# Gate and up products of two feed-forward layers in seven block products instead of eight, and a last norm by features

## What is computed

```python
def rmsnorm(t, g):
    tf = t.astype(jnp.float32)
    y = tf * lax.rsqrt(jnp.mean(tf * tf, axis=-1, keepdims=True) + EPS)
    return (y * g.astype(jnp.float32)).astype(t.dtype)
...
        hffn = modulate(rmsnorm(x, g_norm2[l]), shift2, scale2)
        a, u = jnp.split(jnp.einsum('bsd,df->bsf', hffn, w_ffn_in[l]), 2, axis=-1)
        x = x + gate2[:, None, :] * jnp.einsum('bsf,fd->bsd', jax.nn.silu(a) * u, w_ffn_out[l])

    return rmsnorm(x, g_final)
...
        h = rmsnorm_2(x, norm_ffn[l])
        x = x + (jax.nn.silu(h @ w_ffn_gate[l]) * (h @ w_ffn_up[l])) @ w_ffn_down[l]
    return rmsnorm_2(x, norm_final)
```

## Time and profile before

| | |
|---|---|
| median of 3 runs | 1884.28 us (1883.42 to 1884.56) |
| the profiled execution | 1884.31 us |
| its span, first to last instruction | 1882.5 us |
| TensorE matmul busy | 1847.2 us, 98% |
| TensorE weight load busy | 1435.2 us, 76% |
| VectorE busy | 833.8 us, 44% |
| ScalarE busy | 681.7 us, 36% |
| GpSimd busy | 570.5 us, 30% |
| granted TensorE clock | 0.996 of full |

### The profile page before, as it was taken

How to read it: one execution, slowest core, us unless ns; L and a number is a source line. 1 busy time by engine, 2 the same in 40 slices (tenths; PEclk the granted TensorE clock), 3 DMA queues, 4 the chain that set the end, 5 groups by cost and what they waited for, 6 DMA issues and landing times.

```text
span 1882.5 us, 21005 instructions
## 1 busy us (share of the span) xinstructions
PE 1847.2 (98%) x8472; PEld 1435.2 (76%) x8472; DVE 833.8 (44%) x1232; ACT 681.7 (36%) x1007; POOL 570.5 (30%) x437
## 2 busy tenths in 40 slices
PE   5999999999999999999999999999999999999998
PEld 3777778878777777877888888877776788888886
DVE  6666561425151303334333333548777654423433
ACT  4555552223232323433221222535546532212323
POOL 4643344646365544431000000044556211100100
PEclk9999999999999999999999999999999999999999
DMA  7422112534443122333422322432221222223321
GB/s 286 146 68 68 59 59 95 202 134 164 149 135 112 64 71 85 129 99 90 133 82 91 111 90 70 110 95 80 89 90 57 79 90 89 90 91 92 106 84 54
DMA packets 153299, 192.37 MB, mean 102 GB/s; under 512 B 10297, under 2 KB 130377, under 8 KB 152818
## 3 DMA queue, kind: packets, MB, share of 16 engines
q1 hardware_dynamic: 151202, 181.77, 29.4%
q0 software_dynamic: 1104, 5.24, 1.0%
q10 hardware_dynamic: 896, 4.01, 0.6%
HBM read 188.89 MB, written 4.72 MB: 103 GB/s over the span
## 4 chain that ended last, share of the span: by engine, by line
PE 93%; DVE 4%; ACT 2%; issue 1%; DMA 0%; ACTq 0%; SPq 0%; DVEq 0%
PE bank L1478 26%; PE bank L1483 25%; PE bank L1480 25%; PE bank L1503 2%; PE bank L1501 2%; PE bank L1499 2%; PE bank L1578 2%; PE bank L1512 2%; DVE stg L1794 1%; PE bank L1528 1%; PE bank L1548 1%; PE bank L1564 1%; DVE left L1824 1%; PE bank L1727 1%; PE bank L1706 1%
## 5 line engine op out<-in xcount | busy, mean ns | idle before, releaser
L1478 PE MATMUL bank<-hH,wh 128*128 128x512 f32 x1264 | 519.5, 411 | 3.3 <-ACT hH L2186 3.0
L1483 PE MATMUL bank<-hL,wh 128*128 128x512 f32 x1264 | 501.7, 397 | 0.1
L1480 PE MATMUL bank<-hH,wl 128*128 128x512 f32 x1264 | 501.1, 396 | 0.0
L2573 POOL TENSOR_TENSOR wl<-stg,wh 128x512 fp32r<-128x512 f32 x150 | 202.5, 1350 | 772.8 <-ACT wh L2212 772.6
L2212 ACT ACTIVATE wh<-stg 128x1024 fp32r<-128x1024 f32 (+2 forms) x292 | 298.7, 1025 | 270.2 <-PE bank L1483 190.5
L1478 PEld LDWEIGHTS bank<-hH,wh 128*128 128x128 f32 x1264 | 238.4, 189 | 76.4 <-issue 23.3
L1483 PEld LDWEIGHTS bank<-hL,wh 128*128 128x128 f32 x1264 | 238.3, 189 | 58.2 <-DVE hL L1938 0.5
L1480 PEld LDWEIGHTS bank<-hH,wl 128*128 128x128 f32 x1264 | 239.0, 189 | 53.8 <-issue 2.6
L1785 DVE TENSOR_TENSOR wl<-stg,wh 128x1024 fp32r<-128x1024 f32 (+2 forms) x142 | 168.3, 1188 | 239.8 <-ACT wh L2212 239.3
L2574 POOL TENSOR_TENSOR wl<-stg,wh 128x512 fp32r<-128x512 f32 x150 | 204.2, 1361 | 0.0
L1478 PE MATMUL bank<-h2H,wh 128*128 128x512 f32 x352 | 140.6, 399 | 0.0
(11 more groups left out here) (319 smaller groups left out, 2525.4 us busy)
## 6 DMA issues: line engine op xcount, KB each, us to landing
stg<-in_w_in SPq DMA_DIRECT2D x54, 1024.0 KB, 5.2
stg<-in_w_ada_t SPq DMA_DIRECT2D x48, 512.0 KB, 4.4
stg<-in_w_ffn_in SPq DMA_DIRECT2D x22, 1024.0 KB, 5.1
stg<-in_w_ffn_gate SPq DMA_DIRECT2D x11, 1024.0 KB, 5.3
stg<-in_w_ffn_up SPq DMA_DIRECT2D x11, 1024.0 KB, 5.3
stg<-in_w_ffn_down SPq DMA_DIRECT2D x10, 1024.0 KB, 5.1
stg<-in_w_proj_ret SPq DMA_DIRECT2D x8, 1024.0 KB, 5.1
stg<-in_w_out SPq DMA_DIRECT2D x8, 1024.0 KB, 5.2
```

The costliest lines, as they stand in the source:

```text
L1478: T.matmul(ps, wh, xh, start=j["first"] and k == 0, stop=False)
L1480: T.matmul(ps, wl, xh, start=False, stop=False)
L1483: t = T.matmul(ps, wh, xl, start=False, stop=j["stop"] and last)
L2573: G.tensor_tensor(lo[:, 0:h, :], src[:, 0:h, :], hi[:, 0:h, :], ALU.subtract)
```

## The change

Of the 44 blocks of gate and up weights, the first gate and the first up block of each layer stay as they were. The other 40 (called groups) are done as two by two blocks. A group's weights are cut into four corners of 512 input features (the even or the odd tiles) by 128 output features, the activations into four quarters of 512 input features by 256 tokens. Seven products of a corner, or of a sum of corners (S1 to S4), with a quarter, or a sum of quarters (T1 to T4), stand in place of eight. Each product is 4 tiles of input features times 3 matmuls of 256 columns, 84 matmuls in a group in place of 48 of 512 columns.

- The sums T1 to T4 are made once in each layer (`combine`: VectorE, 128x1024 each, with high and low part), from an unsplit copy of the activations (`HF`, named `ha` and `hb`), which ScalarE writes in 8 more operations of 128x512 in each layer.
- VectorE makes S1 to S4 of each group (128x512 each) into three PSUM banks of rings Z and C. The weight parts `wh` and `wl` are now six buffers of 128x512, one for each product's weights: the high part by ScalarE, the low part by GpSimd for plain corners (products 1, 2 and 4) and by VectorE for sums (3, 5, 6 and 7).
- Products 1, 6, 7 and 4 of a group pile up in one half bank ("own"), and between them VectorE adds what stands there to what ScalarE copied from products 2, 3 and 5 ("other" bank). So product 6 may begin when VectorE has read the bank after product 1, and so on. Own products of one group alternate with products 2, 5 and 3 of the next, or, at a lot's end, with the first down jobs.
- silu, the factor `RT` and the product of gate and up run on rows of 512 tokens, of which the second row is done in halves of 256.
- The down products of tag "b" have features on the partitions as in tag "a". The 32 transposes, `XT` and the norm by rows are gone. ScalarE squares each feature tile, VectorE adds the squares, a matmul with a constant matrix gives the mean, two ScalarE operations of 128x512 give the factor (`factor("n5")`), and `y` scales eight tiles: six on VectorE, two on GpSimd. The output leaves the chip as features by tokens and is turned on the host.

The core of the diff:

```diff
+FAST = "ab"
+QUADS = {1: "11", 2: "12", 3: "S4", 4: "22", 5: "S1", 6: "S2", 7: "S3"}
...
+    def combine(tag):
+
+        for i in range(1, 5):
+            p.tick("v_t", "T", tag, i)
+            emit("combo", tag, i)
+            yield
+            p.split_high(("T", tag), i)
+            emit("combo_high", tag, i)
+            yield
+            yield
+            p.split_low(("T", tag), i, "dve")
+            emit("combo_low", tag, i)
+            yield
...
+        def fast(lot, groups, tail):
+
+            items = [(groups[0], 2), (groups[0], 5), (groups[0], 3)]
+            for g, nxt in zip(groups, groups[1:] + [None]):
+                for e, (own, other) in enumerate(((1, 2), (6, 5), (7, 3))):
+                    items += [(g, own), (nxt, other) if nxt is not None else tail[e]]
...
+            def prepare():
...
+                for which in {5: (1,), 3: (2, 4), 7: (3,)}.get(m, ()):
+                    add(g, which)
+                p.quads[g, m] = {"u": len(p.units)}
+                p.units.append(("quad", g, m))
+                p.n_hi += 1
+                p.quads[g, m]["hi"] = p.n_hi
+                emit("quad_high", g, m)
+                state["low"] = (g, m)
...
+            def product(g, m):
+                if m == 1:
+                    take("G", ("own", g), 0)
+                elif m == 2:
+                    take("G", ("other", g), 0)
+                for k in range(KT // 2):
+                    emit("mult", g, m, k)
+                    p.slot()
+                p.gemms += 1
+                p.mults[g, m] = p.gemms
+                if m == 4:
+                    emit_out(g, 2)
+                    give(("own", g))
+                    return
+                if m != 3:
+                    p.tick("v_c" if m in (1, 6, 7) else "a_c", "C", g, m)
+                emit("part", g, m)
+                if m == 3:
+                    give(("other", g))
+                if m == 6:
+                    emit_out(g, 1)
...
+            halves = [(f2, x0) for f2 in range(4) for x0 in (0, nf // 2)]
+            if groups:
+                halves[1], halves[2] = halves[2], halves[1]
+            for f2, x0 in halves:
+                b = p.block(wd, f2 * 256, k0=f0 + x0, kn=nf // 2)
+                for half in range(2):
+                    p.job(b, half, down_job(lot, 2 * f2 + half, x0, x0 == 0, x0 > 0), x=("f" + tag, lot),
+                          x0=x0, n=nf // 2, first=x0 == 0, stop=x0 > 0, lo=lo)
...
-        WH = [sb(f"wh{i}", [P, 1024], F32R) for i in range(3)]
-        WL = [sb(f"wl{i}", [P, 1024], F32R) for i in range(3)]
+        WH = sb("wh", [P, 6, S], F32R)
+        WL = sb("wl", [P, 6, S], F32R)
...
+            def mult(g, m, k):
...
+                t_of = {4: 4, 5: 1, 6: 2, 7: 3}.get(m)
+                if t_of is None:
+                    c0 = 256 if m == 3 else 0
+                    tile, of_x = 2 * k + (m != 1), (x, 2 * k + (m != 1))
+                    xh, xl = (y[:, c0:c0 + 256] for y in operand(x, tile))
+                else:
+                    of_x = ("T", tag), t_of
...
+                        ticked(pe, "C", g, {6: 1, 7: 6, 4: 7, 5: 2, 3: 5}[m])
+                pe.wait_ge("w_hi", quads[g, m]["hi"])
+                high_done(pe, *of_x)
+                T.matmul(ps, wh[:, k, :], xh, start=k == 0 and m in (1, 2, 5), stop=False, skip_group_check=True)
+                pe.wait_ge(*quads[g, m]["lo"])
+                T.matmul(ps, wl[:, k, :], xh, start=False, stop=False, skip_group_check=True)
+                low_done(pe, *of_x)
+                t = T.matmul(ps, wh[:, k, :], xl, start=False, stop=k == KT // 2 - 1, skip_group_check=True)
+                if k == KT // 2 - 1:
                     t.then_inc(s["gemm"], 1)
...
+            def combo(tag, i):
...
+                out, x, y = {1: (F[:, 0], b12, b11), 2: (F[:, 1], b22, F[:, 0]), 3: (F[:, 0], b22, b12),
+                             4: (F[:, 0], b21, F[:, 1])}[i]
...
+            def sum_(g, which):
...
+                if which == 1:
+                    x, y, op = corner(g, 1, 2), corner(g, 2, 2), ALU.add
+                elif which == 2:
+                    ticked(ve, "S", g, 1)
+                    ve.wait_ge("w_hi", quads[g, 5]["hi"])
+                    x, y, op = sum_of(g, 1), corner(g, 1, 1), ALU.subtract
+                elif which == 3:
+                    x, y, op = corner(g, 1, 1), corner(g, 1, 2), ALU.subtract
+                else:
+                    ticked(ve, "S", g, 2)
+                    x, y, op = corner(g, 2, 1), sum_of(g, 2), ALU.subtract
+                V.tensor_tensor(sum_of(g, which), x, y, op).then_inc(s["v_s"], 1)
+
+            def quad_low(g, m):
+                if QUADS[m][0] == "S":
+                    src, hi, lo = quad_of(g, m)
+                    ve.wait_ge("w_hi", quads[g, m]["hi"])
+                    V.tensor_tensor(lo, src, hi, ALU.subtract).then_inc(s["w_lo_dve"], 1)
...
+            def part(g, m):
+
+                if m in (1, 6, 7):
+                    other = {1: 2, 6: 3, 7: 5}[m]
+                    ve.wait_ge("gemm", mults[g, m])
+                    if m == 6:
+                        emptied(ve, ("other", g))
+                    else:
+                        ticked(ve, "C", g, other)
+                    V.tensor_tensor(kept(g, other), half_of(g, m), kept(g, other), ALU.add).then_inc(s["v_c"], 1)
...
+            def out_row(g, row):
+                x, dst = groups[g], row_of(g, row)
+                if x["which"] == "u":
+                    ticked(ve, "out", x["mate"], row)
+                    if row == 1:
+                        ticked(ve, "C", g, 6)
+                        V.tensor_tensor(dst[:, :], dst[:, :], TMP[4 + 2 * (g % 2)][:, :], ALU.mult).then_inc(s["v_f"], 1)
+                    else:
+                        emptied(ve, ("own", x["mate"]))
+                        ve.wait_ge("gemm", mults[g, 4])
+                        V.tensor_tensor(dst[:, 0:256], half_of(g, 4), dst[:, 0:256], ALU.mult).then_inc(empty(("own", g)), 1)
+                        ticked(ve, "C", g, 7)
+                        V.tensor_tensor(dst[:, 256:512], dst[:, 256:512], kept(g, 5), ALU.mult).then_inc(s["v_f"], 1)
+                elif x["tag"] == "b" and row == 2:
+                    row_free(ve, g, row)
+                    ve.wait_ge("gemm", mults[g, 4])
+                    V.tensor_tensor(dst[:, 0:256], half_of(g, 4), RT[:, 0:256], ALU.mult).then_inc(empty(("own", g)), 1)
+                    ticked(ve, "C", g, 7)
...
+            def y():
+                r5 = factor("n5")
+                for f in range(2, KT):
+                    emptied(ve, ("down", "b", 1, f))
+                    t = V.scalar_tensor_tensor(XR[:, f, :], XR[:, f, :], C("norm_final_2", f), r5[:, :], ALU.mult, ALU.mult)
...
+                    if key == "n5":
+                        A_.activation(RT[:, :], log[:, :], ACTF.Exp, scale=-0.5).then_inc(s["a_r5"], 1)
+
+            def y_scale(f):
+                emptied(ac, ("down", "b", 1, f))
+                A_.activation(TMP[f][:, :], XR[:, f, :], ACTF.Copy, scale=C("norm_final_2", f)).then_inc(s["a_y"], 1)
...
+            def quad_high(g, m):
+                src, hi, _ = quad_of(g, m)
+                q = QUADS[m]
+                if q[0] == "S":
+                    ticked(ac, "S", g, 4 if q == "S2" else int(q[1]))
+                else:
+                    landed(ac, g)
+                released(ac, quads[g, m]["u"] - 6)
+                A_.activation(hi, src, ACTF.Copy).then_inc(s["w_hi"], 1)
...
+            def part(g, m):
...
+                    x = groups[g]
+                    ac.wait_ge("gemm", mults[g, m])
...
+                    t = A_.activation(kept(g, m), half_of(g, m), ACTF.Copy)
+                    t.then_inc(empty(("other", g)) if m == 3 else s["a_c"], 1)
...
+            def row_scale(g, row):
+                dst = row_of(g, row)
+                ticked(po, "silu", g, row)
+                G.tensor_tensor(dst[:, :], dst[:, :], RT[:, :], ALU.mult).then_inc(s["p_f"], 1)
...
+            def y():
+                po.wait_ge("a_y", 2)
+                po.wait_ge("a_r5", 1)
+                for f in range(2):
+                    G.tensor_tensor(XR[:, f, :], TMP[f][:, :], RT[:, :], ALU.mult).then_inc(s["p_y"], 1)
```

582 lines of the change are left out of this document (388 added, 194 removed).

## The result

The changed kernel takes 1957.03 us (median of 4 runs, 1956.37 to 1958.87), the kernel before 1884.42: ratio 1.039, interval 1.038 to 1.040. 1848 was forecast, 1836 to 1886 the range. It is 72.6 us slower where 36 us less were expected: 109 us lie between.

A forecast was written before the change was run, and what follows sets the result against it. TensorE was taken as the bound, with VectorE nearly as busy and setting the second layer's pace. Ten pairs a layer, 199 + 210 = 409 against 450.0 us, save 41.0; 1884.3 - 41.0 + 4.4 = 1847.7, say 1848 us, range 1836 to 1886.

The forecast's parts named there:

- TensorE's step: Start to start of 256-column matmuls in gate and up groups: 0.1172 us taken, 3360 x 0.1172 = 393.8 us, 56.2 less.
- A fixed cost: Rival: a fixed cost in each matmul makes the 256-column step 0.126 us, 1872 us in all; 20%.
- no addition at all: Rival: the 256-column step is 0.111 us and VectorE sets the pace in both layers, 1835 us; 5%.
- loads that don't hide: Slower rival: weight loads no longer hide under matmuls; 1943 us at a step of 0.150, about 2070 at 0.188; 13%.
- 0.2 us a pair for bunches: First layer's pairs of groups: allowance for TensorE waiting on VectorE's readings, added to TensorE's 19.7 us a pair.
- 5% of idle time: Second layer's pairs: VectorE sets the pace, its in-order list of 20.0 us plus 5% for waits gives 21.0 us.
- The slack of 1.4 us: Block products: TensorE waits on VectorE's readings one product ahead, leaving 12 x 0.117 = 1.4 us.
- GpSimd's hold: VectorE operations reading two tiles outside PSUM are delayed by GpSimd: 1.6 us a pair in the first layer, 2.7 in the second.
- The edits around: Outside block products: transposes -3.5, down products +0.6, sums T1 to T4 and lot openings +2, end +5.3; sum +4.4 us.
- The end: From the last matmul's end to the span's end: 12.0 us in place of 6.7, 5.3 us more.
- VectorE or its quarrel with GpSimd costs more: Rival: waits double and stall each group, 21.0 us a pair in the first layer, 22.5 in the second, 1874 us; 13%.
- near 90%: Sign in the changed profile: VectorE's busy share in the second layer, where it was to set the pace.

The follow-up runs named there:

- Experiments 1, 5 and 6: Changed kernel with weight sums one item earlier (1927.7 us); with ScalarE's half of finished rows one product later (1947.48 us); with both (1905.29 us).
- spread: Experiment 7's kernel with VectorE's sums S2 and S4 moved behind the next group's first reading and preparations spread evenly: 1889.36 us.
- experiment 7: Kernel with both moves of experiment 6, plus the first down block's high and low part prepared ahead of each lot's end: 1887.45 us.
- halves: Seven products in both layers, first layer ordered as in experiment 7, second as in spread, with GpSimd's low parts in two operations of 256 columns: 1875.54 us.
- tail_only: Changed kernel with both FFNs in whole products as before, only the last down product and last norm changed: 1879.54 us.

## Why the prediction was wrong

- **TensorE's step, right.** 0.1172 us was taken; the median is 0.117. A fixed cost, no addition at all and loads that don't hide, on which three rivals and 38% hung, did not come up. The prediction named this step as what it would be wrong in above all, with "all else" at a fifth of it; all of the error lay in that rest. The estimate by the Trainium skill (TensorE: Matmul & The Clock Gate, Back-to-back issue gap), 109 ns, was 8 ns low.
- **The sentence that failed:** "In the first layer I allow 0.2 us a pair for bunches", and "I add 5% of idle time" in the second. It adds each engine's work, takes the longest, and leaves a small allowance for lists that wait for each other. Measured, a pair takes 168 x 0.1172 = 19.7 us and on top 37.2 / 10 = 3.7 us in the first layer, 58.0 / 10 = 5.8 in the second: 23.4 and 25.5 in place of 19.9 and 21.0. That is 80 us of the 109. Experiments 1, 5 and 6 show that 52 us go by another order of the same work.
- **The slack of 1.4 us** was named, but its readings were set against VectorE's mean load, not against what stands ahead of them: a low part and two sums (2.1 us), or on ScalarE a high part that waits for its sum, or a SiLU that waits for GpSimd (2.01 us).
- **GpSimd's hold:** 16 + 27 = 43 us were priced into VectorE's list, as work. Cutting GpSimd's low parts took 26 us off VectorE's busy time in the changed kernel and 46 in spread, and 30 and 25 us off the kernel's. The size was fair, its place not: in the first layer it was put where TensorE's work would hide it, and it came as waits in both.
- **The edits around: one term missing, one too small.** The end of each lot was costed at nothing and took 19.3 us in all; experiment 7 took such waits away. The openings were given 2 us; they took 20.4 where the kernel before has 7.9 in both layers, so 10.5 more than given. 1847.7 + 80.0 + 19.3 + 10.5 = 1957.5, and the small terms left about cancel (the first FFN began 2.7 us earlier, the stage between was 1.4 longer).
- **The end, right:** 12.0 forecast (the terms as written add up to 11.9), 12.0 measured:

```profile
1942.94 0.40 PE L1748 MATMUL bank<-fLb,wh 128*128 128x512 f32 x1
...
1947.30 4.04 DVE L2520 SCALAR_TENSOR_TENSOR XR<-XR,col,bank 128x512 f32<-128x512 f32 x6 [3.23 <-ACT bank L2685]
```
- **The rivals.** The one that came was "VectorE or its quarrel with GpSimd costs more", at 1874 us, in kind but not in size: 21.0 and 22.5 us a pair against 23.4 and 25.5. No rival had lists that wait for each other while no engine is full. That mechanism should have been the rival on the slower side, in place of loads that don't hide.
- **What was to show it:** VectorE "near 90%" in the second layer is about 70%; this alone contradicts the working. The steps over 0.3 us at products' starts are there, more of them in the second layer, and so are sums of 1.7 us and the chain through VectorE, but ScalarE is named as often as VectorE.

## What to carry to other kernels

When an edit halves the slack between a producer and the reading that lets it go on, sums of work say little: write down, for each reading, what stands ahead of it in its in-order list and whether one of those waits for another engine, and compare that with the slack. Put the operation that TensorE waits for ahead of preparations, and make an operand that another engine turns over one item before it is turned over. A saving on the busiest engine is real only once such chains fit: here 56 us of matmuls were 8 us of the two FFN stages and 4 of the whole kernel, against the version with the new end alone (halves and tail_only), and 7 of the 8 came in the layer with less side work. And when an order is mended, look at which engines now work at the same moment: the new orders ran VectorE more often into GpSimd's hold.
